# Out-projection taken into the expert ring, with a normalisation in one shifted pass

## The reference, cut to what matters

```python
def layer_norm(x, g, b):
    mu = mean(x); var = mean((x - mu) ** 2)
    return (x - mu) * rsqrt(var + 1e-5) * g + b

def finish_layer(x, y_rwkv, y_attn, w_o, ln1_g, ln1_b, peer_wq, ...):
    mix = concatenate([y_rwkv, y_attn]) @ w_o          # 2048 x 2048
    x = layer_norm(ALPHA * x + mix, ln1_g, ln1_b)      # ALPHA = 2 ** 0.25
    return layer_norm(ALPHA * x + peer_ffn(x, peer_wq, ...), ln2_g, ln2_b)

def peer_ffn(x, wq, subkeys, u_tab, v_tab):
    q = x @ wq                                         # then top keys, gates
    ...                                                # gelu(x @ u_e), times gates, @ v_e
```

## Time and profile before

| what | value |
|---|---|
| median of three runs | 3363.21 us (3360.62 to 3365.99) |
| the profiled execution's own time | 3360.29 us |
| its span | 3358.6 us |
| PE busy / DVE busy / ACT busy | 88% / 57% / 32% of the span |
| mean granted clock of PE | 0.906 of full speed |

### The profile page before, as it was taken

One profiled execution on the slowest core, in us unless ns is written; L12 is line 12 of the kernel. 1 busy time (PEld: TensorE's weight loads), 2 busy tenths in 40 slices (PEclk: granted clock), 3 DMA queues, 4 the chain that ended last, 5 costly groups with the idle time before them and its releaser, 6 DMA issues. The chain is left out here.

```text
span 3358.6 us, 52683 instructions
## 1 busy us (share of the span) xinstructions
PE 2963.3 (88%) x21616; PEld 2664.3 (79%) x21616; DVE 1920.0 (57%) x3373; ACT 1085.1 (32%) x1302; POOL 249.9 (7%) x357
## 2 busy tenths in 40 slices
PE   3999848999984788596999999999999999999996
PEld 2999817788761333295999999999999999999995
DVE  3444346666646752244899999666664444445544
ACT  1222211111111111122444433455554433344442
POOL 0000000000012101000000000122221110000000
PEclk7999958989886557798999999999999999999998
DMA  2444300000014404341555455799988777755551
GB/s 112 159 154 158 125 13 11 11 21 11 14 55 114 151 2 164 140 166 66 178 170 177 166 172 179 272 337 325 344 320 309 285 277 250 246 185 184 185 180 66
DMA packets 145176, 541.79 MB, mean 161 GB/s; under 512 B 25177, under 2 KB 45378, under 8 KB 113826
## 3 DMA queue, kind: packets, MB, share of 16 engines
q1 hardware_dynamic: 109586, 400.11, 34.6%
q0 software_dynamic: 35376, 138.70, 11.6%
HBM read 521.85 MB, written 16.80 MB: 160 GB/s over the span
## 5 line engine op out<-in xcount | busy, mean ns | idle before, releaser
L2252 DVE TENSOR_TENSOR px_w_r<-px_w,px_wh 128x2048 fp32r<-128x2048 f32 x272 | 623.0, 2291 | 463.2 <-ACT px_wh L2040 461.5
L2040 ACT ACTIVATE px_wh<-px_w 128x2048 fp32r<-128x2048 f32 x272 | 520.9, 1915 | 901.8 <-PE px_bank L256 732.1
L254 PE MATMUL px_bank<-pe_high,px_wh 128*128 128x256 f32 (+1 forms) x2304 | 658.5, 286 | 30.3 <-DVE px_w_r L2252 30.2
L255 PE MATMUL px_bank<-pe_low,px_wh 128*128 128x256 f32 (+1 forms) x2304 | 655.5, 285 | 0.0
L256 PE MATMUL px_bank<-pe_high,px_w_r 128*128 128x256 f32 (+1 forms) x2304 | 651.5, 283 | 0.0
L254 PEld LDWEIGHTS px_bank<-pe_high,px_wh 128*128 128x128 f32 x2304 | 437.6, 190 | 57.7 <-issue 50.5
L255 PEld LDWEIGHTS px_bank<-pe_low,px_wh 128*128 128x128 f32 x2304 | 436.4, 189 | 0.0
L256 PEld LDWEIGHTS px_bank<-pe_high,px_w_r 128*128 128x128 f32 x2304 | 434.2, 188 | 0.0
L254 PE MATMUL px_pair<-px_arena_gh,px_wh 128*128 128x256 f32 x1024 | 292.0, 285 | 14.5 <-DVE px_arena_gl L2259 13.4
L254 PE MATMUL px_bank<-px_arena_gh,px_wh 128*128 128x256 f32 x1024 | 291.6, 285 | 8.6 <-DVE px_arena_gl L2259 8.5
L255 PE MATMUL px_pair<-px_arena_gl,px_wh 128*128 128x256 f32 x1024 | 290.9, 284 | 0.0
(11 more groups left out here) (460 smaller groups left out, 5128.7 us busy)
## 6 DMA issues: line engine op xcount, KB each, us to landing
px_w<-in_peer_u SPq DMA_DIRECT2D x128, 1024.0 KB, 4.9
px_w<-in_peer_v SPq DMA_DIRECT2D x128, 1024.0 KB, 6.0
in_w<-in_w_in SPq DMA_DIRECT2D x49, 1024.0 KB, 4.8
out_w<-in_w_o SPq DMA_DIRECT2D x16, 1024.0 KB, 4.8
px_w<-in_peer_wq SPq DMA_DIRECT2D x16, 1024.0 KB, 4.9
px_lay_u_x<-x_rows POOLq DMA_DIRECT2D x32, 512.0 KB, 5.9
px_arena_u_x<-x_rows POOLq DMA_DIRECT2D x32, 512.0 KB, 5.9
pq_pages<-in_kv_pages SPq DMA_DIRECT2D x48, 256.0 KB, 7.8
```

The costliest lines, as they stand in the source:

```text
L254: pe.matmul(out, w_high, high, start=start, stop=False, skip_group_check=True)
L255: pe.matmul(out, w_high, low, start=False, stop=False, skip_group_check=True)
L2040: act.activation(w_high[t % 2][:], w[t % SL][:], ACT.Copy).then_inc(raised, 1)
L2252: v.tensor_tensor(w_low[t % SL][:], w[t % SL][:], w_high[t % 2][:], ALU.subtract) \
```

## The change

The phases "rest", "mix", "out" and "ln1" go. Their work becomes part of `peer_experts`: the tile list begins with 16 tiles ("o", c), one for each chunk of w_o, so that all other tiles have numbers higher by 16.

- Tile 0 is loaded in four quarters of 512 columns; ACT and DVE split the mixers' output and tile 0 quarter by quarter in turn, and product 0 waits for its quarters.
- x is loaded (`x_in`, in memory that the gates take later) by SP between tiles 1 and 2.
- Behind product c, DVE adds the bank to ALPHA * x (`move`). The mean over the features of chunk 0 alone, a first guess at the row's mean, is taken by one ones-product behind product 1 (`shift_sum`) and subtracted from each chunk (`center`). DVE sums the chunks (`total_chunk`), ACT squares them (`square_chunk`) and DVE sums the squares (`total_square`), all while later products run.
- Behind product 15 two ones-products of the totals give mean and mean square of the shifted values (`norm_sums`), and `norm_scale` the factor.
- Then, by groups of four chunks: DVE multiplies by the factor and adds an offset (`spin`), ACT scales and shifts with g and b and raises the result (`bend`, `raise_x`), DVE lowers it (`lower_x`), and PE makes that quarter of product 16, the first query tile.

The diff, cut to its core (declarations of tiles and semaphores are left out; there are 19 new semaphores):

```diff
-            cx.phase(load, "rest", ((xT[:], x_rest[:, :, META:N]),))
...
-            cx.phase(split, "mix", mixT[:, :, META:N], high, low)
-            cx.phase(project, "out", KT, a["w_o"], high, low,
-                    lambda v, c, acc: v.scalar_tensor_tensor(xT[:, c, :], xT[:, c, :], ALPHA, acc,
-                                                             ALU.mult, ALU.add))
-
-            cx.phase(layer_norm, "ln1", xT, ln_gb[:, 1], ones, into=mixT[:, :, META:N])
...
-    tiles, u = [], 0
+    tiles, u = [("o", c) for c in range(KT)], 0
...
SP
+                    if t == 0:
+                        for k in range(4):
+                            sp.dma_start(w[0][:, 512 * k:512 * k + 512].rearrange("p (k e) -> p k e", e=P),
+                                         a["w_o"][0][:, 4 * k:4 * k + 4, :]).then_inc(quarter_in[k], 16)
+                    elif x[0] == "o":
+                        if t == 2:
+                            sp.dma_start(x_in, x_rest).then_inc(x_loaded, 16)
+                        sp.dma_start(w[s][:].rearrange("p (k e) -> p k e", e=P), a["w_o"][x[1]]) \
+                            .then_inc(loaded[s], 16)
...
ACT
+                def raise_quarter(k):
+                    act.wait_ge(quarter_in[k], 16)
+                    act.activation(w_high[0][:, 512 * k:512 * k + 512], w[0][:, 512 * k:512 * k + 512], ACT.Copy) \
+                        .then_inc(quarter_high, 1)
+                def square_chunk(c):
+                    act.wait_ge(centered, c + 1)
+                    act.activation(square[c % 2], xT[:, c, :], ACT.Square).then_inc(squared, 1)
+                def bend(k):
+                    act.wait_ge(spun, k + 1)
+                    for c in range(4 * k, 4 * k + 4):
+                        ins = act.activation(xT[:, c, :], xT[:, c, :], ACT.Identity, scale=gb[:, 0, c:c + 1],
+                                             bias=gb[:, 1, c:c + 1])
+                    ins.then_inc(bent, 1)
+                    act.wait_ge(bent, k + 1)
+                    raise_x(k)
...
                 for k in range(4):
+                    raise_x(k)
+                    raise_quarter(k)
                 raise_tile(1)
                 for t, x in enumerate(tiles):
+                    if x[0] == "o" and t:
+                        square_chunk(t - 1)
+                    if t == KT - 1:
+                        square_chunk(KT - 1)
                     if t + 2 < NT:
                         raise_tile(t + 2)
...
+                    if t == KT - 1:
+                        root()
+                        for k in range(4):
+                            bend(k)
...
PE
                     for k in range(KT):
+                        if t == 0 and k % 4 == 0:
+                            pe.wait_ge(quarter_low, k // 4 + 1)
+                            pe.wait_ge(x_low, k // 4 + 1)
+                        if t == KT and k % 4 == 0:
+                            pe.wait_ge(x_low, 5 + k // 4)
...
+                def shift_sum():
+                    pe.wait_ge(moved, 1)
+                    pe.matmul(bank[6][:, 0:NY], ones[:], xT[:, 0, :], start=True, stop=True).then_inc(shift_done, 1)
+                def norm_sums():
+                    pe.wait_ge(x_total, 1)
+                    pe.matmul(bank[4][:, 0:NY], ones[:], total_x, start=True, stop=True).then_inc(mean_done, 1)
+                    pe.wait_ge(sq_total, 1)
+                    pe.matmul(bank[5][:, 0:NY], ones[:], total_sq, start=True, stop=True).then_inc(power_done, 1)
...
+                    if t == 1:
+                        shift_sum()
+                    if t == KT - 1:
+                        norm_sums()
...
DVE
+                def move(c):
+                    v.wait_ge(used, c + 1)
+                    if c == 0:
+                        v.wait_ge(x_loaded, 16)
+                        v.wait_ge(x_low, 4)
+                    ins = v.scalar_tensor_tensor(xT[:, c, :], x_in[:, c, :], ALPHA, bank[c % SL][:, 0:NY], ALU.mult, ALU.add)
...
+                def norm_scale():
+                    v.wait_ge(mean_done, 1)
+                    lk(v.tensor_copy(shift, bank[4][:, 0:NY]))
+                    lk(v.tensor_tensor(offset, shift, shift, ALU.mult))
+                    v.wait_ge(power_done, 1)
+                    lk(v.scalar_tensor_tensor(rstd, bank[5][:, 0:NY], LN_EPS, offset, ALU.add, ALU.subtract))
+                    v.reciprocal(rstd, rstd).then_inc(inv_done, 1)
...
+                def spin(k):
+                    x = xT[:, 4 * k:4 * k + 4, :]
+                    lk(v.tensor_tensor(x, x, rstd.rearrange("p (o t) -> p o t", o=1).to_broadcast([P, 4, NY]), ALU.mult))
+                    v.tensor_tensor(x, x, offset.rearrange("p (o t) -> p o t", o=1).to_broadcast([P, 4, NY]), ALU.add) \
+                        .then_inc(spun, 1)
+                def mix_chunk(c):
+                    move(c)
+                    if c == 1:
+                        take_shift()
+                        center(0)
+                        total_chunk(0)
+                    if c:
+                        center(c)
+                        total_chunk(c)
+                        total_square(c - 1)
...
                 for k in range(4):
+                    lower_x(k, 0)
+                    lower_quarter(k)
                 v.wait_ge(small_in, 16)
                 lower_tile(1)
                 for t, x in enumerate(tiles):
+                    if x[0] == "o":
+                        mix_chunk(t)
+                    if t == KT - 1:
+                        total_square(KT - 1)
+                        norm_scale()
...
                         lower_tile(t + 2)
...
+                    if t == KT - 1:
+                        norm_offset()
+                        for k in range(4):
+                            spin(k)
+                            if k:
+                                lower_x(k - 1, 1)
+                        lower_x(3, 1)
```

More of the change, by code:

```diff
@@ L1833, in place_plan, with peer @@
     return first, after, done, ahead
-def peer(cx, a, xT, ident):
+def peer(cx, a, xT, ident, x_rest, gb, ones):
     nc = cx.nc
@@ L1844, in peer, with peer_experts @@
         low = st.enter_context(nc.sbuf_tensor("pe_low", [P, KT, NY], F32R))
-        cx.phase(peer_experts, a, xT, ident, high, low, g_rest, x_rows)
-def peer_experts(cx, a, xT, ident, high, low, g_rest, x_rows):
+        cx.phase(peer_experts, a, xT, ident, x_rest, gb, ones, high, low, g_rest, x_rows)
+def peer_experts(cx, a, xT, ident, x_rest, gb, ones, high, low, g_rest, x_rows):
     nc = cx.nc
@@ L1863, in peer_experts @@
         w_high = [sb(f"wh{s}", [P, 2048], F32R) for s in range(2)]
+        x_in = gates[:].rearrange("p e t -> p (e t)")[:, 0:KT * NY].rearrange("p (k t) -> p k t", t=NY)
         picks = sb("picks", [P, 3, NY])
@@ L1875, in peer_experts @@
         xrows = lay("xrows", [TS, D])
+        lay.used = 0
+        square = [lay(f"square{k}", [P, NY]) for k in range(2)]
+        total_x, total_sq, shift, rstd, offset = (lay(x, [P, NY]) for x in ("total_x", "total_sq", "shift", "rstd", "offset"))
         lay.used = 0
@@ L1955, in peer_experts, with arrived @@
         G = EH // E2
+        def arrived(t):
+            return 16 * (t // SL + (t % SL > 0))
         def step_number(hf, k):
@@ L2040, in raise_tile, with raise_x, root @@
                     act.activation(w_high[t % 2][:], w[t % SL][:], ACT.Copy).then_inc(raised, 1)
+                def raise_quarter(k):
+                    act.wait_ge(quarter_in[k], 16)
+                    act.activation(w_high[0][:, 512 * k:512 * k + 512], w[0][:, 512 * k:512 * k + 512], ACT.Copy) \
+                        .then_inc(quarter_high, 1)
+                def raise_x(k):
+                    act.activation(high[:, 4 * k:4 * k + 4, :], xT[:, 4 * k:4 * k + 4, :], ACT.Copy).then_inc(x_high, 1)
+                def square_chunk(c):
+                    act.wait_ge(centered, c + 1)
+                    act.activation(square[c % 2], xT[:, c, :], ACT.Square).then_inc(squared, 1)
+                def root():
+                    act.wait_ge(inv_done, 1)
+                    act.activation(rstd, rstd, ACT.Sqrt).then_inc(rstd_done, 1)
+                def bend(k):
[6 more added lines that the diff above has]
+                    raise_x(k)
                 def raise_gates(t):
@@ L2134, in product @@
                 def product(t):
-                    pe.wait_ge(lowered, t + 1)
-                    n = NY if tiles[t][0] == "q" else ND
+                    if t:
+                        pe.wait_ge(lowered, t)
+                    n = NY if tiles[t][0] in "oq" else ND
                     if t >= SL and t - SL in freed:
@@ L2248, in _, with lower_quarter, lower_x @@
                 lk = Link(v, link)
+                def lower_quarter(k):
+                    v.wait_ge(quarter_high, k + 1)
+                    v.tensor_tensor(w_low[0][:, 512 * k:512 * k + 512], w[0][:, 512 * k:512 * k + 512],
```

(43 more changed lines are left out.)

39 lines of the change are left out of this document (17 added, 22 removed).

## The result

The changed kernel takes 3313.24 us (median of 4 runs, 3309.63 to 3321.77) where the kernel before takes 3361.91 beside it (4 runs, 3355.47 to 3365.99): ratio 0.9861, interval 0.9836 to 0.9885. A second measurement gives 3320.04 against 3364.24, ratio 0.9865 (0.9843 to 0.9887). The forecast was 3317, between the two. The profiled execution has a span of 3310.7 us (run 3312.37), 47.9 less than before.

What follows compares the result with a forecast made beforehand. Waits at both edges of the out-products were the bound, TensorE within them. Gains 19.1 + 27.2 less 1.1 take 45.2 us off the 3358.6 us span: 3313.4, or 3317 timed; range 3307 to 3330.

Steps and rivals of the forecast that it cites:

- The front: Attention's end to product 15's end: first product at 1407.7 instead of 1429.98, end 1515.4 against 1534.52, gain 19.1 us (16 to 22).
- one of my signs of being wrong: At the start of the out-products: quarters of tile 0 landing later than 2.5 us would show the prediction wrong.
- The out-tiles: Tiles 3 to 15: 6.40 us each at clock 1.00, DVE's steps hidden beside the products with 2.1 us to spare.
- The slower rival: Tiles 3 to 15: each starts behind a gap and the clock drops, 7 us a tile, 91 us, 3408 in all; chance 3%.
- The tail: Product 15's end to tile 17, the norm and product 16: 31 us (29 to 34) against 58.2, gain 27.2 us.
- Starved start: Rival at the first loads: quarters and x_in share the engines badly, quarters 2.3 us late, 8 us in all, 3325; chance 10%.
- reloaded tables: Rival in the tail: ACT reloads tables before each bend's Identity and raise_x's Copy, 10 us, 3327; chance 7%.
- no change: Rival in the later stages: the ring gives the time back later, so the total stays; chance 3%.
- Semaphores: End of the expert phase: 19 more semaphores cleared at 0.06 us each give back 1.1 us.

Runs made afterwards that it cites:

- the second profile: The changed kernel profiled and timed again with the same code, against the kernel before: 3320.04 us against 3364.24, ratio 0.9865 (0.9843 to 0.9887).

## Why the prediction was right

**The front.** The first quarter came 1.5 us later than I had it (7.06 us after the attention's end, not 5.6): a 256 KB piece at the head of the burst took 3.9 us from its issue, where I had scaled 2.5 between the 1.8 and 4.8 of the earlier trace rows. That was one of my signs of being wrong, and it came true. So product 0 starts at +8.47, not +6.9. It cost nothing at the end: product 2 waits for tile 2, which landed at +20.6 (forecast +20.0), and it starts at +24.93 (forecast +24.2), behind a gap of 0.92 us instead of 1.7 and without the fall of the clock that I had added (0.8). Errors of 0.7 and 0.8 cancel, and product 15 ends at +114.75 against +114.6. Part of the agreement is luck. I had no term for tile 1 landing late; by the second profile it is worth up to 2.5 us, inside the range. Product 0 starts 20.7 us earlier than before. The run with one load gives 4.0 of that to the quarters; how the rest divides between the separate load of x, two phase boundaries and the wait for w_o, no run shows.

**The out-tiles.** 6.40 us a tile, clock 1.00, DVE's steps 0.46 at 0.49, spare time 2.03 against the 2.1 forecast. The run with three more steps shows it as slack.

**The slower rival** had its threshold right, as far as 1.5 and 4.4 us enclose it, and its price wrong (its terms also add up to 3409, not 3408): I let a gap cost 2.1 us and then 48 matmuls at the low clock, 7 us a tile. With the slack overrun in all tiles it was 2.2 us a tile, close to DVE's excess alone (4.4 - 2.03 = 2.4). Where DVE set the pace, the slow stretch of TensorE came out of the wait that followed (1.94 us, then 0.44). The Trainium skill (TensorE: Matmul & The Clock Gate, HAM oscillation) tells of a kernel in which each burst behind a wait starts throttled. Behind 12.84 us of idle time product 16 does so (0.61 and 0.44 us a matmul); the burst behind 2.39 us does too (0.61 us for its first matmul). Behind gaps of 0.44 and 1.94 us no burst does; the fall came 0.5 to 1.0 us into five of the six bursts behind 1.94 us.

**The tail.** norm_offset starts at 7.85 (forecast 8.2, its steps having cost 0.46 as put), the four bursts at 16.0, 19.9, 23.8 and 27.3 (forecast 15.9, 19.9, 24.0, 27.0). The first burst hides two errors that cancel: norm_offset came 0.35 us early, and the bend's four Identities took 2.18 us where I had 4 x 0.48 = 1.92. The end was mis-sized: I held the last 12 matmuls and 1 us of tile 17 at the low clock; the clock came back at 1544 and the last burst took 1.95 us instead of 3, so 29.28 instead of 31. The runs confirm each piece: norm steps beside the products 22.2, quarter waits 7.5, pointer columns 1.3, the lowering of tile 17 in the way 1.5, beside what the clock did to the last burst.

**Starved start, reloaded tables, no change.** The first happens in part and is mostly paid for, as above; the table load stands once ahead of the root and not among the bends; and the ring gives nothing back. Its 3.2 us less is no gain of the change: the same stretch took 1718.63 in the second profile.

**Semaphores.** 1.04 us for 19 shown, 1.1 forecast; the boundary itself is 0.4 longer than that.

## What to carry to other kernels

A phase that keeps one engine waiting can be moved beside a phase that has the other engines to spare: sum the steps per tile, set them against the idle time in front of the step that they delay, and the answer is a threshold (here 2.03 us a tile), nothing before it and the excess after it. In a serial tail read each engine's written order: one 2.23-us step for a later tile ahead of a dependent one was worth 1.5 us. A single profile's total hides effects of this size; compare stage by stage, and read the untouched stages first for their scatter.

## What the runs showed of the hardware that was not expected

Loads issued in order by one queue don't land evenly from one execution to the next. The 1 MB behind four 256 KB quarters was there no later than 12.3 us after the attention's end in the first profile and at 14.65 in the second, with the same code; in the runs whose first loads were the same it came at 13.7, at 13.6, or by 12.7.

The clock's fall did not follow from the length of a gap alone. Behind 0.92 us, ahead of product 2, it stayed at 1.00. Behind 1.99 us, ahead of product 1 in the second profile, and behind 1.94 us with nine more steps it fell 0.5 to 1.0 us into the burst and stayed low for some 3 us (0.44 us a matmul), but behind one of the six gaps of 1.94 us not at all. Behind 2.39 us the burst began low. In the tail it stayed at full speed behind 2.07 us when tile 17 was lowered late:

```profile
1536.74 0.40 PE L254 MATMUL px_bank<-pe_high,px_wh 128*128 128x288 f32 x1 [2.07 <-DVE pe_low L2319]
```

After the tail's 12.84 us the clock stayed low over three bursts and into the fourth, but not equally far: the last burst took 1.95 us in the first profile and 2.35 in the second, with the same code. When tile 17 was lowered late, one burst was enough (0.40 us for the first matmul of the second).
